# Rotary swap and gate row by DMA instead of matrix products, one table reduction later, and narrower waits before the scores

## The reference, cut to what matters

```python
mod = silu(c) @ w_ada + b_ada                       # 6 vectors of 1024
shift1, scale1, gate1, shift2, scale2, gate2 = split(mod)
h = rmsnorm(x, g) * (1 + scale1) + shift1
proj = h @ w_in                                     # pool inputs, q, k, v, two gates
# rotation: only the first 16 of the 64 rows of each head, in two groups of 8
def rope(x1, x2, rest): return [x1*cos - x2*sin, x1*sin + x2*cos, rest]
attn = softmax(mask(rope(q) @ rope(k).T / 8)) @ v   # 8 heads
merged = g_pool * (pooled @ w_branch_pool) + g_attn * (attn @ w_branch_attn)
x = x + gate1 * (merged @ w_out)
# then: 128 expert rows (u, v) per token gathered from tables of 16384 rows
x = x + gate2 * peer_ffn(modulate(x, shift2, scale2))
# second block: 16 heads (8 with a forget gate, 8 in bands), then a conv FFN
```

## Time and profile before

| what | value |
|---|---|
| time, median of three runs | 1173.78 us (1173.57 to 1175.6) |
| the profiled execution, its own time | 1174.26 us |
| its span in the profile | 1172.4 us |
| PE busy | 1041.2 us (89%) |
| DVE busy | 826.7 us (71%) |
| ACT busy | 423.2 us (36%) |
| POOL busy | 290.3 us (25%) |
| DMA over the span | 390.46 MB, mean 333 GB/s |

### The profile page before, as it was taken

How to read it: one execution, slowest core, us unless ns; L and a number is a source line. 1 busy time by engine, 2 the same in 40 slices (tenths; PEclk the granted TensorE clock), 3 DMA queues, 4 the chain that set the end, 5 groups by cost and what they waited for, 6 DMA issues and landing times.

```text
span 1172.4 us, 13740 instructions
## 1 busy us (share of the span) xinstructions
PE 1041.2 (89%) x5066; PEld 702.4 (60%) x5066; DVE 826.7 (71%) x1912; ACT 423.2 (36%) x895; POOL 290.3 (25%) x262
## 2 busy tenths in 40 slices
PE   5999999898999996886886878788899999999997
PEld 3799976644555543432332323333389878999986
DVE  5699765768767768778887555555566878888843
ACT  3545622322332222222222111111266665665631
POOL 0000001444354543353544444445000000000000
PEclk8999999999999998898988999989999999999999
DMA  9977594999999999899999999999994443554530
GB/s 367 427 319 297 239 399 158 418 401 422 420 419 420 421 422 421 365 410 421 422 421 421 422 421 422 420 422 422 384 396 180 145 179 134 198 209 163 197 144 37
DMA packets 48199, 390.46 MB, mean 333 GB/s; under 512 B 5498, under 2 KB 5890, under 8 KB 7300
## 3 DMA queue, kind: packets, MB, share of 16 engines
q0 software_dynamic: 37040, 269.51, 55.5%
q1 hardware_dynamic: 11092, 120.07, 26.1%
HBM read 388.50 MB, written 1.06 MB: 332 GB/s over the span
## 4 chain that ended last, share of the span: by engine, by line
PE 52%; DMA 31%; DVE 11%; ACT 3%; issue 2%; POOL 1%; SPq 1%; DVEq 0%
DMA ring<-in_uv,idx 27%; PE ps L1457 18%; PE ps L1801 15%; PE ps L1958 5%; DMA ring<-in_w_ada 4%; DVE ring L1243 3%; PE ps L1669 2%; PE ps L1611 2%; PE ps L1886 2%; PE ps L1481 1%; PE ps L1684 1%; DVE ring_r L885 1%; POOL ring L514 1%; PE ps L1510 1%; DVE ring L896 1%
## 5 line engine op out<-in xcount | busy, mean ns | idle before, releaser
L1801 PE MATMUL ps<-ring,probT 128*128 128x512 f32 x1020 | 490.7, 625 | 103.6 <-ACT probT L759 102.1
L1243 DVE CUSTOM_DVE_ANT_0 ring<-h2t,ring 128x1024 f32<-128x1024 f32 x255 | 308.7, 1222 | 166.0 <-DMA ring<-in_uv,idx 165.8
L1801 PEld LDWEIGHTS ps<-ring,probT 128*128 128x128 f32 x1020 | 192.6, 199 | 338.8 <-issue 194.7
L514 POOL DMA_INDIRECT ring<-in_uv,idx x255 | 287.9, 1129 | 339.1 <-PE ps L1801 287.0
L1457 PE MATMUL ps<-util_r,ring_r 128*128 128x256 f32 x1312 | 216.9, 282 | 0.0
L1457 PEld LDWEIGHTS ps<-util_r,ring_r 128*128 128x128 f32 x1312 | 181.6, 189 | 1.3 <-issue 1.1
L885 DVE TENSOR_TENSOR ring_r<-ring,ring_r 128x1024 fp32r<-128x1024 f32 x134 | 157.7, 1220 | 34.0 <-ACT ring_r L536 33.9
L754 ACT ACTIVATE prob<-prob 128x2 f32<-128x2 f32 (+2 forms) x98 | 20.0, 204 | 368.5 <-DVE prob L1243 368.4
L536 ACT ACTIVATE ring_r<-ring 128x1024 fp32r<-128x1024 f32 x134 | 133.6, 1050 | 41.5 <-DMA ring<-in_w_in 19.3
L1457 PE MATMUL ps<-h_r,ring_r 128*128 128x256 f32 x704 | 126.1, 282 | 0.1
L759 ACT ACTIVATE probT<-ct,prob 128x128 f32<-128x128 f32 x256 | 85.5, 392 | 76.5 <-DVE prob L1249 75.8
(11 more groups left out here) (213 smaller groups left out, 980.4 us busy)
## 6 DMA issues: line engine op xcount, KB each, us to landing
ring<-in_w_in SPq DMA_DIRECT2D x12, 2048.0 KB, 13.8
ring<-in_w_up SPq DMA_DIRECT2D x11, 2048.0 KB, 7.9
ring<-in_w_ada SPq DMA_DIRECT2D x7, 2048.0 KB, 9.8
ring<-in_w_down SPq DMA_DIRECT2D x6, 2048.0 KB, 7.7
ring<-in_w_ada SPq DMA_DIRECT2D x8, 1024.0 KB, 16.4
ring<-in_w_out SPq DMA_DIRECT2D x4, 2048.0 KB, 8.0
ring<-in_w_q SPq DMA_DIRECT2D x3, 2048.0 KB, 11.3
ring<-in_w_br SPq DMA_DIRECT2D x2, 2048.0 KB, 13.1
```

The costliest lines, as they stand in the source:

```text
L514: e.indirect_dma_start(out=row_buf[n], out_offset=None, in_=uv, in_offset=bass.IndirectOffsetOnAxis(ap=idx[:, tt, k:k + 1], axis=0)).then_inc(
L1243: e.tensor_tensor_reduce(u, h2t[:, tt, :], u, 1.0, 0.0, ALU.mult, ALU.add, av[:, tt, n % 128:n % 128 + 1]).then_inc(*made.put(("dot", n)))
L1801: ins = e.matmul(acc[half][:, :], diag[:, n % 8, :], row_buf[n][:, D + half * 512:D + (half + 1) * 512], start=(k == 0), stop=(k == 127))
```

## The change

PE's rotation products and PE's gate products go. Instead POOL clears the two scratch areas early, and once ACT has copied q (later k), issues four small transfers each that bring the swapped groups of 8 rows into the scratch area; DVE multiplies from there, with the sign now in the sine table. POOL writes the eight columns of `gate1` to DRAM, and reads them back as one row for every partition. On DVE, `ada(6)` and quarters 14 and 15 go ahead of the rotation, and `ada(5)` goes from in front of the rotation of k to the first round of heads, in front of `ada(7)`. In the second block PE waits for the second units of q and k only in round 2.

```diff
         def gpsimd(e):
             pool = Engine(e)
 
+            pool.wait_ge(acted, ("row squares", 1, 1, 1))
+            for name in ("q", "k"):
+                e.memset(rope_of[name][1], 0.0).then_inc(*cleared.put(name))
+            def swap(name):
+                x3, scratch = rope_of[name]
+                pool.wait_ge(cleared, name)
+                for h in (0, 64):
+                    for a, b in ((h, h + 8), (h + 8, h)):
+                        e.dma_start(scratch[a:a + 8], x3[b:b + 8]).then_inc(*swapped[name].put((a, b)))
+            pool.wait_ge(acted, unit("in", 1, 2))
+            swap("q")
+            pool.wait_ge(acted, unit("in", 2, 2))
+            swap("k")
+            pool.wait_ge(made, "mod2")
+            e.dma_start(gate_row.rearrange("(k p) -> p k", p=P), mod[:, 16:24],
+                        allow_slow_non_contiguous=True).then_inc(*spread_gate.put("out"))
+            pool.wait_ge(spread_gate, "out")
+            pool.wait_ge(done, ("quarter", 35))
+            e.dma_start(gate1, gate_row.rearrange("(o n) -> o n", o=1).broadcast_to([P, D])).then_inc(*spread_gate.put("in"))
...
-                    dve.wait_ge(done, ("rope", name, j0))
+                    dve.wait_ge(swapped[name], (72, 64))
...
             ada(4)
-            split_low(12, 13)
+            split_low(*range(12, 16))
+            ada(6)
             rope("q")
-            split_low(14, 15)
-            ada(6)
             split_low(16, 17)
-            ada(5)
+            rope("k")
             split_low(18, 19)
-            rope("k")
...
                 normed(1, 2 * s)
                 normed(1, 2 * s + 1)
+                if s == 0:
+                    ada(5)
                 if s in (0, 2):
                     ada(7 + s // 2)
...
             pe.wait_ge(acted, unit("in", 1, 2))
-            rope("q")
             columns("in", 2, 2, xs, lambda k: [], acted)
             tokens("in", 3, 0, xs, lambda k: [])
             pe.wait_ge(acted, unit("in", 2, 0))
             pe.wait_ge(acted, unit("in", 2, 2))
-            rope("k")
             tokens("in", 3, 2, xs, lambda k: [])
...
-            for half in range(2):
-                o = group(("gate1", half))
-                pe.wait_ge(made, "mod2")
...
-            pe.wait_ge(acted, unit("in2", 0, 2))
             pe.wait_ge(acted, unit("in2", 1, 0))
             o = group("own sums")
...
-            pe.wait_ge(made, unit("in2", 1, 2))
             for s in range(9):
+                if s == 2:
+                    pe.wait_ge(acted, unit("in2", 0, 2))
+                    pe.wait_ge(made, unit("in2", 1, 2))
```

More of the change, by code:

```diff
@@ L214, in build @@
 def build(nc, x_in, c_in, consts, bands_in, bmask_in, cols, relb, rows, w_ada, w_in, w_pool, w_br, w_out, w_q, keysT, uv, w_in2, w_f2,
-          w_out2, w_up, w_down, out, sums):
+          w_out2, w_up, w_down, out, sums, gate_row):
     with ExitStack() as ctx:
@@ L362, in build @@
         spread_sums = Mark(sem("s_sums"), 16)
+        spread_gate = Mark(sem("s_gate1"), 16)
+        swapped = {name: Mark(sem(f"s_swapped_{name}"), 16) for name in ("q", "k")}
+        cleared = Mark(sem("s_cleared"))
         stored = Mark(sem("s_stored"), 16)
@@ L368, in build @@
         made = Mark(sem("s_dve"))
-        marks = [*loaded, *half_loaded.values(), *once.values(), *arrived_in.values(), spread_sums, stored, high, low, done, acted, made]
+        marks = [*loaded, *half_loaded.values(), *once.values(), *arrived_in.values(), spread_sums, spread_gate, *swapped.values(), cleared, stored, high, low, done, acted, made]
         where = {}
@@ L914, in rope @@
                     xs, ss = x3[:, j0:j0 + 2, :], scratch[:, j0:j0 + 2, :]
-                    dve.wait_ge(done, ("rope", name, j0))
+                    dve.wait_ge(swapped[name], (72, 64))
                     dve.wait_ge(once["ct2"], 0)
-                    e.tensor_tensor(ss, pair(("rope", name, j0)), K("sinm").unsqueeze(1).broadcast_to([P, 2, T]),
+                    e.tensor_tensor(ss, ss, K("sinm").unsqueeze(1).broadcast_to([P, 2, T]),
                                     ALU.mult).then_inc(*made.put(("sin", name, j0)))
@@ L969, in rows_added @@
                         dve.wait_ge(done, ("mix1", tt, half))
-                        dve.wait_ge(acted, ("gate1", 1))
+                        dve.wait_ge(spread_gate, "in")
                     else:
@@ L1491, in tokens @@
                         banks.give(("tokens", i, tt), acted if kind == "in" else made, ("v", i, tt))
[L1493 to L1500, removed]
             def pair_scores(att, i):
@@ L2021, in constants @@
             cosm[h + m], cosm[h + 8 + m] = cos[m], cos[m]
-            sinm[h + m], sinm[h + 8 + m] = sin[m], sin[m]
+            sinm[h + m], sinm[h + 8 + m] = -sin[m], sin[m]
             rot[h + 8 + m, h + m] = -1.0
@@ L2118 @@
     sums = nc.dram_tensor("sums", (8, T), F32, kind="Internal").ap()
-    build(nc, *args, out, sums)
+    gate_row = nc.dram_tensor("gate_row", (D,), F32, kind="Internal").ap()
+    build(nc, *args, out, sums, gate_row)
     r = run(nc, [arrays], core_ids=[0])
```

## The result

The changed kernel takes 1195.62 us (median of 4 runs, 1194.54 to 1196.03); the kernel before took 1173.76 us beside it. The ratio is 1.0181, with a 95% interval of 1.0164 to 1.0199. The prediction said 1181, with a range of 1177 to 1187: the sign was right, the size was not. The profiled execution took 1195.24 us, with a span of 1193.4.

The account below looks back on a forecast made before the run. PE was taken to bound the kernel up to 187 us and from 895 us, the gathers' DMA between. Against 1174.26 us: + 8.0 (wait) + 1.7 (clock) - 1.7 (gate) - 1.0 (second block) = 1181.3, said as 1181, range 1177 to 1187.

Parts of the forecast that it names:

- The wait ahead of the products by v: First heads: DVE idles for the load of ada 7, so PE multiplies by v 8.0 us later, net of rotation's gain.
- Is the swap in time?: Ahead of the first heads: k's swap lands at 76.2 us, PE does not wait for the rotation; first mask at 83.5.
- The third rival: Rotation of k: swap lands late, counting from a landing after 77.4 us; up to 6.5 us more, 1187.3; chance 0.08.
- The clock: Behind PE's wait at the products by v: some 3.3 us of work at 1.2 GHz, + 1.7 us (bounds 0 and 3.4).
- The gate row: PE's gate products ahead of the mix: 1.7 us saved, row in time within 23.8 us of cover, no wait.
- If it takes DMA time from ada 11: Gate row's write beside ada 11's load: DVE's merges come later, price 0 to 2.5 us, taken as 0.
- The fourth rival: DVE's use of the gate row: it comes late if its chain exceeds 23.8 us; up to 11.7 more, 1192.5; chance 0.07.
- The rotation's gain of 2.5 us: Ahead of the first heads: 3.08 us of PE products go, 0.83 returns as waiting; first scores start 2.47 us earlier.
- The second block: Second block's first scores: PE's 1.01 us wait for DVE's copy of k's second half goes, 1.0 us less at the end.

Follow-up runs that it names:

- both costs undone: Changed kernel with `ada(5)` back ahead of the first heads and the gate row's write issued early, swaps and narrowed waits kept: 1171.93 us, ratio 0.9997.

## Why the prediction was wrong

**The wait ahead of the products by v: right in kind, + 12.1 where the sum had + 8.0.** The chain itself was as described: `ada(5)` starts 4.70 us behind the first mask, ada 7 is issued as it ends, lands after 7.7 us (7.6 taken), and DVE stands idle for 7.71. The failing step is "Is the swap in time?": the first mask came at 87.40 and not at 83.5, 3.9 us late, and 12.1 - 3.9 = 8.2. It was late because DVE could start the rotation of k only at 81.25, where the sum had the swap landed at 76.2; these are 5.0 us, 1.2 of them covered. They have three parts. The copy of k was 1.5 us late (72.06 against 70.54), since the load of in 4 took 16.9 us instead of 15.3; PE waited 2.56 us for that copy, where I had 0.83. POOL's issues took 1.7 us less than I had. And the landing took 5.2 more: I took 1.6 us from the 8 KB row, a transfer that had the queues nearly to itself; beside in 5's load the last of the four pieces landed 6.8 us after its issue. The held-back load shows it from the other side, with 3.5 us for that piece. The third rival had named this wait, down to the landing after 77.4 from which it counts (81.25 - 77.4 = 3.85), and I gave it 0.08; the reason that I named there, DVE locking POOL out, is not what these traces show. Why in 4 landed late no run isolates. The swap of q ran beside it, and from the load's issue to its first conversion the nine kernels with that swap took 15.8 to 16.9 us (mean 16.4), the three without 14.7 to 15.3 (mean 15.1).

**The clock: right, with some luck.** + 1.7 was taken, and 13.8 - 12.1 = 1.7 measured, at the lower level for some 3 us behind the wait. The same products behind the same wait lost 1.6 to 2.0 us in four of the other kernels, and 2.8 in that with the write early, where the lower level lasted until some 117 us. A second stretch followed, which the sum lacked: behind the 7.20 us ahead of the mix its 40 products took 19.15 us against 17.33 before, 1.8 more.

**The gate row: wrong, and the largest miss.** - 1.7 was taken, + 5.6 + 1.8 came: PE's products went as computed, and 7.20 us of wait and 1.8 of clock followed (19.4 - 13.8 = 5.6 = 7.2 - 1.7, rounded). The failing step is "If it takes DMA time from ada 11 ... the price is 0 to 2.5 us; I take 0". I bounded what the load could lose by its own excess over the full rate, as if a transfer of 4 KB could take no more from its neighbours than that. The load lost 19.0 - 9.8 = 9.2 us. The fourth rival had the landing (1.6 to 18 us; 13.8 measured), but looked for the cost at the wrong reader: the row, read back by 184.7 us, was in time for DVE at 192.65, and the load beside it was not. Even so that rival's condition was met. From `mod` (158.55) to the row are 26.1 us, over the 23.8 of cover, and only the late ada 11 hid it, which put DVE's use 34.1 us behind `mod`. (The upper end of its sum adds to 35.7, not 35.5.)

**The rotation's gain of 2.5 us: not there.** The changed kernel hides this, but with both costs undone nothing is left of it that the medians can tell. I had read that PE alone bounds the stretch. But the two rotations stand at 58.8 and 71.8 us, and the chain runs through PE only from 85 us on. Ahead of that the chain of before runs through DVE, which had no pause from 56.35 us to the first mask:

```profile
76.28 1.13 DVE ring L896
...
84.37 0.70 DVE area L922
```

PE waited 0.22 us for DVE there, and that row says that DVE would be the bound as soon as PE got shorter. The order of the change that would have used the gain is the one that cost 16 to 17 us.

**The second block: right.** - 1.0 taken, the wait of 1.01 us is gone in every trace that has the edit.

**What is left.** From the load of in 4's issue to the first gather, which takes out the drift of the start, the traces have 144.9 us before, 166.2 after, 151.3 with `ada(5)` back, 157.8 with the gate by products, and 144.4 with both. So, on top of the swaps and narrowed waits, the late `ada(5)` costs 13.4 us there (157.8 - 144.4), the write 6.9 (151.3 - 144.4), and both 21.8, 1.5 more than the sum. The medians have 12.2, 6.3 and 23.5, 5 more than the sum, of which 1.2 can be the two occasions. The rest lies behind the first gather, where the kernels with the narrowed waits, whose code is the same there, took 970.6 to 974.0 us to the end, and the one before 974.2. Within that spread is also what I read there in this pair: 1.9 us later between the gathers and the second block's own sums (this stretch takes 693.5 to 697.3 us in the twelve traces), and 1.0 us back in the up part, whose 1056 products take 125.19 us instead of 126.16. The second is no gain of the change but the clock: PE waits 2.05 us for DVE there in all twelve traces, and behind it the lower level was granted in three of them, the one before, that with both costs undone and that with in 5 held back; these three take 277.3 to 277.5 us from the second block's first scores to the end, the nine others 276.4 to 276.5. With them 12.1 + 1.7 - 1.7 + 7.2 + 1.8 + 1.9 - 1.0 - 1.0 = 21.0, the difference of the spans. What spreads the stretch of the gathers by up to 3.8 us stays open.

## What to carry to other kernels

Take the price of a small transfer from a row that has the same company: the queues' state at its issue decides, and what it does to the loads beside it can cost more than its own landing. A strided write of single elements was such a case here at 4 KB; lay it out in runs or issue it when no load is in flight. And before an engine is relieved, look where the chain of waits runs at that very place, and at the shortest wait in the engine's list: the engine named there is the next bound, and the gain ends at it. When two uses of one buffer move together on an engine, the load between them has no cover left, and its whole landing is a stall.

## What the runs showed of the hardware

A write of 4 KB from 128 partitions to DRAM in pieces of 4 bytes landed 9.4 us after its issue with the queues otherwise empty (two kernels; 9.9 in a third, where a load was issued in its last 0.5 us), 13.8, 14.3 and 12.7 beside a 2 MB load (the changed kernel, that with `ada(5)` back and that with in 5 held back), and that load then took 19.0, 17.6 and 18.1 us instead of 9.8. The same bytes in pieces of 32 landed in 6.3 us and left the load at 10.6. The records hide it: the profile shows 32 packets on POOL's queue for either form, and in the window of the early write the DMA share is next to nothing:

```profile
139.00:141.00 2.00, 2.00 (x19) 2.00 (x18) 2.00 (x3) 1.26 (x2) 0.00 (x0) 1.00 0.06 1
```

Low GB/s beside pending loads, as at 166 to 168 us above, is how such a write looks. The DMA share does not tell: it was 0.06 there, but 1.05 at 98 GB/s from 154 to 156 us in the kernel with `ada(5)` back. Four swaps of k, each 8 partitions by 4 KB, landed in 2.0 us (median; the last one 3.5) with the load of in 5 held back and in 4.3 to 6.0 us beside it.

Whether the clock falls behind a short wait was not decided by the wait. Two kernels, `ada(5)` back and both costs undone, at the same place:

```profile
71.30 7.41 PE L1502 MATMUL ps<-ring_r,util_r 128*128 128x256 f32 x48 [2.22 <-ACT area L567]
```
```profile
71.17 5.84 PE L1506 MATMUL ps<-ring_r,util_r 128*128 128x256 f32 x48 [2.20 <-ACT area L568]
```

In the first the granted clock was 0.56 and 0.58 from 72 to 76 us, in the second 1.00, for 1.6 us of difference. Of nine kernels that waited 1.4 to 2.6 us there, two fell to the lower level (waits of 2.22 and 2.17 us), and the one with 2.56 us did not.
